# Banded attention as one pipeline over 16 blocks, with pairs of heads on the two halves of the TensorE array

## The reference

```python
def _windowed_gqa(h, pos, w_qkv, sink, w_o):
    qkv = h @ w_qkv
    q, k, v = jnp.split(qkv, [1024, 1280], axis=-1)      # 16 q heads, 4 k heads, 4 v heads, 64 wide
    # per query block of 128 tokens: keys of the block before, its own, the block after
    scores = jnp.einsum('bnqkgd,bnskd->bnkgqs', q * 64 ** -0.5, kb)
    scores = scores - slopes * dist                      # ALiBi by distance of positions
    scores = jnp.where(mask, scores, NEG)                # |t - s| <= 128
    p = jax.nn.softmax(jnp.concatenate([scores, sink_col], axis=-1), axis=-1)[..., :-1]
    return jnp.einsum('bnkgqs,bnskd->bnqkgd', p, vb).reshape(B, S, 1024) @ w_o
```

## Time and profile before

| | |
|---|---|
| Median of 3 runs | 1250.61 us (1248.01 to 1251.63) |
| The profiled execution's own time | 1250.18 us |
| Span of its profile | 1248.4 us, so 1.8 us lie around it |
| TensorE busy | 1191.3 us, 95% |
| VectorE, ScalarE, GpSimd busy | 630.4, 354.0, 399.0 us |
| Mean granted TensorE clock | 0.990 |
| TensorE share of the chain that ended last | 80%, DVE 9% |

### The profile page before, as it was taken

How to read it: one execution, slowest core, us unless ns; L and a number is a source line. 1 busy time by engine, 2 the same in 40 slices (tenths; PEclk the granted TensorE clock), 3 DMA queues, 4 the chain that set the end, 5 groups by cost and what they waited for, 6 DMA issues and landing times.

```text
span 1248.4 us, 18246 instructions
## 1 busy us (share of the span) xinstructions
PE 1191.3 (95%) x5796; PEld 992.8 (80%) x5796; DVE 630.4 (50%) x1067; ACT 354.0 (28%) x689; POOL 399.0 (32%) x415
## 2 busy tenths in 40 slices
PE   6899999999999999999889999899999999999996
PEld 5788878788888888888867777678788888888885
DVE  6777764433333433454576776744443333343432
ACT  4266652222200111111365665632222200111101
POOL 3343335333311333343241412325233311323342
PEclk8999999999999999999989999999999999999998
DMA  6211113232433233333200101013333332333421
GB/s 161 68 34 35 35 34 101 85 99 86 119 93 89 87 101 101 109 93 91 70 20 18 36 0 34 18 39 114 97 89 101 103 115 68 101 96 89 120 81 67
DMA packets 176475, 96.67 MB, mean 77 GB/s; under 512 B 8752, under 2 KB 173104, under 8 KB 176432
## 3 DMA queue, kind: packets, MB, share of 16 engines
q1 hardware_dynamic: 176432, 96.12, 26.5%
HBM read 94.01 MB, written 2.10 MB: 77 GB/s over the span
## 4 chain that ended last, share of the span: by engine, by line
PE 80%; DVE 9%; issue 4%; ACT 3%; POOL 2%; DMA 1%; ACTq 0%; DVEq 0%; POOLq 0%; SPq 0%
PE bank L949 26%; PE bank L951 25%; PE bank L950 25%; PE bank L1391 2%; DVE w_lo L1473 1%; POOL w_hi L442 1%; DVE stat L2004 1%; DVE apt_lo L1666 1%; PE bank L1088 1%; DVE s_a L1658 1%; DVE bpt_lo L2009 1%; DMA x_n<-in_x 1%; ACT s_b L880 1%; ACT bpt_hi L886 0%; DVE w_lo L1490 0%
## 5 line engine op out<-in xcount | busy, mean ns | idle before, releaser
L1473 DVE TENSOR_TENSOR w_lo<-w_raw,w_hi 128x1024 fp32r<-128x1024 f32 (+2 forms) x151 | 203.2, 1346 | 297.8 <-POOL w_hi L442 297.7
L442 POOL TENSOR_SCALAR w_hi<-w_raw 128x1024 fp32r<-128x1024 f32 (+3 forms) x159 | 183.3, 1153 | 421.4 <-PE bank L951 410.0
L949 PE MATMUL bank<-x_hi,w_lo 128*128 128x512 f32 x784 | 308.3, 393 | 9.9 <-DVE w_lo L1473 7.7
L951 PE MATMUL bank<-x_hi,w_hi 128*128 128x512 f32 x784 | 306.3, 391 | 0.0
L950 PE MATMUL bank<-x_lo,w_hi 128*128 128x512 f32 x784 | 306.3, 391 | 0.0
L949 PEld LDWEIGHTS bank<-x_hi,w_lo 128*128 128x128 f32 x784 | 147.8, 189 | 42.1 <-DVE w_lo L1473 5.5
L951 PEld LDWEIGHTS bank<-x_hi,w_hi 128*128 128x128 f32 x784 | 147.7, 188 | 30.9
L950 PEld LDWEIGHTS bank<-x_lo,w_hi 128*128 128x128 f32 x784 | 148.0, 189 | 29.7
L949 PE MATMUL bank<-f_hi,w_lo 128*128 128x512 f32 x352 | 137.8, 391 | 1.0 <-DVE f_lo L1776 1.0
L951 PE MATMUL bank<-f_hi,w_hi 128*128 128x512 f32 x352 | 137.1, 389 | 0.0
L950 PE MATMUL bank<-f_lo,w_hi 128*128 128x512 f32 x352 | 137.0, 389 | 0.0
(11 more groups left out here) (219 smaller groups left out, 1863.6 us busy)
## 6 DMA issues: line engine op xcount, KB each, us to landing
w_raw<-in_ffn_w_gu SPq DMA_DIRECT2D x88, 512.0 KB, 3.8
w_raw<-in_ffn_w_down SPq DMA_DIRECT2D x32, 704.0 KB, 4.4
w_raw<-in_a_w_qkv SPq DMA_DIRECT2D x12, 512.0 KB, 3.8
w_raw<-in_a_w_o SPq DMA_DIRECT2D x8, 512.0 KB, 3.6
w_raw<-in_b_w_o SPq DMA_DIRECT2D x8, 512.0 KB, 3.8
w_raw<-in_b_w_in SPq DMA_DIRECT2D x4, 672.0 KB, 4.0
w_raw<-in_b_w_uq SPq DMA_DIRECT2D x4, 576.0 KB, 4.0
x_n<-in_x SPq DMA_DIRECT2D x4, 512.0 KB, 5.3
```

The costliest lines, as they stand in the source:

```text
L442: pool.tensor_scalar(split_part(w_hi, s, cols, kv), raw_part(s, cols, kv), 1.0, 1.0, ALU.mult, ALU.mult) \
L949: pe.matmul(o, ll, rh, start=start, stop=False)
L951: return pe.matmul(o, lh, rh, start=False, stop=stop)
L1473: dve.tensor_tensor(split_part(w_lo, s, cols, kv), raw_part(s, cols, kv), f(split_part(w_hi, s, cols, kv)), ALU.subtract) \
```

## The change

What it does:

- The two loops over groups and query blocks become one list of 16 blocks, b = 4 x group + n. TensorE issues the scores of block b, then the transposes of block b-1, then a few projection steps (`a_filler`), then the values of block b-1 piece by piece, with further steps between. Where n = 0, the second pair of heads is scored behind the transposes. Scores use four banks (0, 1, 2, 7).
- The key tiles are stored without zeros: `ks` holds key heads as the projection left them (even head on partitions 0 to 63, odd on 64 to 127), `kx` the same with the halves exchanged, filled by four DMAs from SBUF to SBUF. A score matmul reads 64 partitions only; the even head's and the odd head's matmuls alternate, so they stand on different halves of the array.
- The query projections 0 and 1 get buffers of their own, loaded right behind the key weights, and run before the value projection. All query tiles are double-buffered (`aq_hi[:, g % 2]`).
- V is projected token block by token block, with all key blocks of the contraction together, into banks 6 and 5, and is written directly to `av_hi` and `av_lo` for all groups at once. The scores of block 0 stand behind its first quarter.
- The low parts of queries 2 to 7 and of three query and output weights move from DVE to POOL. Reciprocals are taken for two heads at once. An early exponential loads ACT's table. The masks `near` are made before the keys are evicted, and lie in unused ends of the weight slots.

```diff
-            def a_group(g, last):
-                def scores(u):
...
-                    q = (slice(None), hd // 2, slice(n * P, (n + 1) * P))
-                    k = (slice(None), hd % 2, slice(k0 * P, (k0 + nk) * P))
-                    product(banks[u % 3][:, 0:nk * P], aq_hi[q], aq_lo[q], kp_hi[k], kp_lo[k], True, True) \
-                        .then_inc(s_done, 1)
...
+            def a_scores(b, i):
...
+                for k_low, q_low in ((False, True), (True, False), (False, False)):
+                    for odd in range(2):
+                        rows = slice(odd * HD, (odd + 1) * HD)
+                        q = (aq_lo if q_low else aq_hi)[rows, g % 2, i, n * P:(n + 1) * P]
+                        here = odd == g % 2
+                        kt = (ks_lo if here else kx_lo) if k_low else (ks_hi if here else kx_hi)
+                        ins = pe.matmul(banks[A_SCORE_BANKS[2 * i + odd]][:, 0:nk * P], q,
+                                        kt[rows, g // 2, k0 * P:(k0 + nk) * P],
+                                        start=q_low, stop=not (k_low or q_low))
+                        if not (k_low or q_low):
+                            ins.then_inc(s_done, 1)
...
+            for b in range(1, A_BLOCKS + 1):
+                n = b % NT
+                nk = a_keys(b - 1)[1]
+                steps = a_filler(b)
...
+                if b < A_BLOCKS:
+                    a_scores(b, 0)
+                    if n:
+                        a_scores(b, 1)
+                if b == A_BLOCKS:
+                    fill(3)
+                elif n == 3:
+                    fill(KD)
+                a_turn(b - 1, 0)
+                a_turn(b - 1, 1)
+                if n == 0 and b < A_BLOCKS:
+                    a_scores(b, 1)
+                fill(2 if b < A_BLOCKS else 1)
+                a_values(b - 1, 0)
+                if nk > 2:
+                    a_turn(b - 1, 2)
+                fill(1)
+                a_values(b - 1, 1)
+                fill(KD)
+                if nk > 2:
+                    a_values(b - 1, 2)
...
+            sp.wait_ge(ks_ready, 2)
+            for src, dst in ((ks_hi, kx_hi), (ks_lo, kx_lo)):
+                for half in range(2):
+                    there, here = slice((1 - half) * HD, (2 - half) * HD), slice(half * HD, (half + 1) * HD)
+                    sp.dma_start(f(dst[there, :, :]), f(src[here, :, :])).then_inc(kx_in, 16)
...
+                if g < GROUPS - 1:
+                    c = C_Q + 2 * g
+                    if n == 3 if g == 0 else n == 2:
+                        a_q_lo(2 * g + 2)
+                        w_split_hi(c // 2 + 1, 0, W_COLS)
+                    if n == 3:
+                        a_q_lo(2 * g + 3)
+                        a_w_lo(c + 2)
+                if g and n == 0:
+                    w_split_hi(C_Q // 2 + g, 1, W_COLS)
```

More of the change, by code:

```diff
@@ new lines, in a_turn @@
+            def a_turn(b, i):
+                unit = a_unit(b, i)
+                if b == 0 and i < 2:
+                    pe.wait_ge(q_tmp_ready, i + 1)
+                else:
+                    pe.wait_ge(pt_free, unit - 1)
+                for j, hd in enumerate((0, 2, 1, 3)):
+                    if i == 0 and j != 2:
+                        pe.wait_ge(p_ready, 4 * b + hd + 1)
+                    last = pe.transpose(banks[3 + unit % 2][:, j * P:(j + 1) * P],
+                                        s_a[:, b % 2, hd, 1 + i * P:1 + (i + 1) * P], ident[:])
+                last.then_inc(pt_done, 1)
@@ new lines, in a_values @@
+            def a_values(b, i):
+                k0, nk = a_keys(b)
+                pe.wait_ge(pt_free, a_unit(b, i) + 1)
+                if i == 0:
+                    pe.wait_ge(o_free, O_A + b)
+                    if b == 0:
+                        pe.wait_ge(av_zero, 2)
+                        pe.wait_ge(v_ready, NT)
+                for odd in range(2):
+                    at = (2 * (b // NT) + 1 - odd) * HD
+                    v = (slice(None), k0 + i, slice(at, at + P))
+                    p = (slice(None), b % 2, i, slice(2 * P * odd, 2 * P * (odd + 1)))
+                    last = product(banks[5][:, 0:2 * P], av_hi[v], av_lo[v], apt_hi[p], apt_lo[p],
+                                   i == 0 and odd == 0, i == nk - 1 and odd == 1)
+                if i == nk - 1:
+                    last.then_inc(o_done, 1)
@@ L1730, in _ @@
-            for g in range(GROUPS - 1):
-                a_group(g, False)
-            a_group(GROUPS - 1, True)
             def add_to_h(c, bank_s, m, used, dst=None):
```

719 lines of the change are left out of this document (352 added, 367 removed).

## The result

The change takes 1261.26 us (median of 6 runs, 1259.48 to 1265.82) beside 1251.12 for the kernel before on the same chip: ratio 1.0086, 95% interval 1.0068 to 1.0103. It is **10 us slower**, where 1246.2 was forecast, and outside the range of 1239 to 1254.

What follows compares the result with a forecast made beforehand. TensorE, busy 95% of the span, was taken as the bound. First stretch 3.5 us less, two middle groups 1.0 less, last group 0.1 more: 1250.18 - 4.4 = 1245.8, median 0.4 higher, so 1246.2; range 1239 to 1254.

Steps and rivals of the forecast that it cites:

- the term for the waits of the new order: Block-by-block walk through the engines' queues in the changed stage: 20.6 us of TensorE waits, each handover counted in full.
- Last group: Blocks 12 to 15: own work 25.6, waits 6.7, output split 0.3, together 32.6 us, 0.1 more than before.
- Blocks with n = 3: Fourth query block of a group: own work 6.9 us, wait of 1.3 for the third transposes' copies before the last values.
- the two weight splits: Block 1: splits on POOL and DVE hold up the maxima and first probabilities, a wait of 3.6 us.
- n = 0: First query block of a group: own work 6.1 us, wait of 0.8 for a weight split moved to POOL.
- n = 1 and 2: Second and third query blocks: own work 6.2 and 7.2 us, wait of 0.9 in each before the values.
- the pairs: Score matmuls of even and odd heads: one spacing a pair, 0.173 or 0.118 us, 13.9 us less.
- the visits: Entering and leaving the half-height mode for scores: 19 times at 0.25 us, 4.8 us in all.
- the copies from SBUF to SBUF: Four new 256 KB key copies before block 0's scores: cost nothing, or 5 us if as slow as loads.
- pairs one after the other: Rival: paired score matmuls do not overlap, scores cost 13.9 us more, total 1255.9, slower; chance 0.12.
- drains: Rival: each entry and exit of half-height mode costs 0.70 us together, +6.8, total 1253.0, no measurable change; chance 0.14.
- The marks named: Signs to check: paired starts, 0.9 us apt_lo waits, block 1 near 53 us, twelfth output product near 175; wrong if groups exceed 31.

Runs made afterwards that it cites:

- the run with the steps around them: The change with half of the projection steps of n = 3 blocks moved from ahead of the transposes to later places: 1257.7 us, ratio 1.0050.
- the run with the heads in turn: The change with each pair's score products issued as three of one head, then three of the other, instead of alternating: 1262.0 us, ratio 1.0089.
- The late split: The change with half the n = 3 projection steps behind the transposes and the second query-weight slot's split behind block 1's maxima: 1255.1 us, ratio 1.0035.
- scores_twice: The change with every pair's three score products computed twice, 14 us more of TensorE's time: 1268.5 us, ratio 1.0138.
- the runs with both pairs ahead: The change with block b+1's scores ahead of block b-1's last values, half the n = 3 steps behind transposes: 1253.6 us; later runs keep both edits.
- the pairs' run in the old order: The kernel before, own order of work kept, only the score products issued in pairs on the two halves of the rows: 1251.9 us, ratio 1.0003.
- the reordered kernel: The change with scores issued earlier and projection steps, weight splits, query readout and output steps moved: 1247.5 us, ratio 0.9969.

## Why the prediction was wrong

- **The step that failed** is the term for the waits of the new order. "My walk has 20.6 us of waits" was too small by some 13 us, of which the clock is about 2. The forecast was 3.9 us a middle group over own work of 26.4; the groups took 34.2 and 32.5, so 7.8 and 6.1. From block 1 to block 4: 33.0 us in place of 28.9. Last group 35.6 in place of 32.6. With 0.4 up to block 1, these make, to rounding, the 13.4 us between the forecast stage (145.7) and the measured one. By place:
  - Blocks with n = 3: the walk waited only for the third copy. All projection steps stand ahead of the transposes, so the first two copies are bare as well; 1.2 to 1.3 us a block over the forecast (blocks 3, 7, 11). Shown by the run with the steps around them for blocks 7 and 11, which got 1.2 shorter; block 3 got 0.4 shorter and block 4 1.4. (The walk's own terms, 0.28 + 0.59 + 0.75 + 0.69 less 0.7, also make 1.6 and not the 1.3 written.)
  - Block 1 took 12.2, not 9.8, of which 1.5 is the clock; without its fall (the run with the heads in turn) it took 10.7, so the two weight splits cost 4.5 in place of 3.6. The late split shows that they are what block 1 waits for.
  - n = 0: block 4 took 8.7, not 6.9, with waits of 1.6 for w_lo and 0.4 for aq_lo; blocks 8 (7.0) and 12 had 0.4 for w_lo. The walk had one subtraction and the split ahead of the scaling of block 4; at the end of group 0 four stand there, two aq_lo, w_hi and w_lo, from 84.73 to 90.59:

```profile
84.73 1.28 POOL L549 TENSOR_TENSOR aq_lo<-q_tmp,aq_hi 128x512 fp32r<-128x512 f32 x1
85.97 1.05 POOL L479 TENSOR_SCALAR w_hi<-w_raw 128x1024 fp32r<-128x1024 f32 x1
86.98 1.29 POOL L549 TENSOR_TENSOR aq_lo<-q_tmp,aq_hi 128x512 fp32r<-128x512 f32 x1
88.21 2.38 POOL L543 TENSOR_TENSOR w_lo<-w_raw,w_hi 128x1024 fp32r<-128x1024 f32 x1
```

  So POOL was late by its queue and not by its speed: its subtractions took the 1.29 and 2 x 1.29 forecast, or less. (The 1.29 and 1.87 of the earlier trace rows are a multiplication and an addition, not subtractions.) Moving w_hi and w_lo ahead cut block 4 by 1.5.
  - n = 1 and 2: right to 0.5 us (7.4 in blocks 5 and 9, 8.6 and 8.5 in 6 and 10, beside 7.1 and 8.1). The 0.66 ahead of block 8's values stands for the 0.9 forecast.
  - The last group's 3.0 us is not broken down. Block 15's fall of the clock is in it: from its scores to the end of the stretch the change takes 15.5 us at a clock of 0.89, scores_twice, with 0.7 us more work there, 15.1 at 1.00.
- **The clock** was in no term. In the run with the heads in turn the same block 1 kept a clock of 1.00 and took 10.7 us, so the fall costs 1.5 there; block 15's costs 0.4 to 1.1 by the comparison above, together 1.9 to 2.6 us, an estimate. In the runs with both pairs ahead block 15's does not occur.
- **What the pairs' run in the old order adds.** It is no proof against the sum, which was for the new order; but it shows where such a saving goes: half into entering and leaving, the rest into waits, here for banks.
- **Right:** the pairs (one spacing, so 13.9 us less), the visits nearly (0.29 beside 0.25, 0.8 us more over 19), block 1 at 53.35 (forecast 53.4), the copies from SBUF to SBUF unseen, V's evictions hidden, the rest of the kernel unchanged within 0.7. The rule of the Trainium skill (TensorEngine Tiling (Array Packing), Key Properties) that a change of mode drains TensorE agrees with the late starts, 0.20 us on entering and 0.09 on leaving. The rivals "pairs one after the other" and "drains" (0.70 a visit) fall. The first had the right sign and, with 1255.9, half of the loss, by a mechanism that isn't there.
- The marks named were met in part: twelfth product at 188.6, not 175; groups over 31 us, which was said to make the forecast wrong.

**Settled:** the loss is order, not work. Moving instructions alone took 14.3 us from the change by the medians and 16.2 from the stretch, at the same count of TensorE's matmuls. **Open:** what the pairs are worth in the reordered kernel. An added 14 us of scores cost 11.8 there, but full-height scores would also save the 19 visits (5.5 us), so some 6 us is an estimate; the reordered kernel with full-height scores was not run. Which chain holds the old order at 30.8 us, with banks enough for the pairs, was not tried either.

## What to carry to other kernels

Before counting an engine's saved time, ask what would hold the order if that engine were faster: the cheap test is to save the time in the old order first, and to look whether the edit that saves it brings waits of its own, as the pairs did here with the banks. In a software pipeline, follow one block around through every in-order queue and ask what the *first* instruction of the next block stands behind: here scores behind the last values, then q_tmp ahead of the maxima, then a weight split ahead of the normalisations. Walk every instruction of each queue: the walk here left two of POOL's out. Whatever waits for another engine belongs behind what is ready, and filler belongs where the waits are, not where the program text has a gap.

## What was not expected of the hardware

Matmuls on different halves of the rows need not be neighbours in the program: three of one head ran beside the three of the next, starts 0.01 us apart, in the same time as when they alternated (0.17 a pair at 384 columns). So did their weight loads: the fourth matmul's began at 55.42, the second's at 55.52. The Trainium skill (PSUM — Partial Sum Buffer, Engine vs sequencer instructions) says that matmuls start and complete in program order; for two sets of rows this trace differs. And the clock's fall after a stall was not the same each time. In the run with the heads in turn block 1 begins 2.06 us later in the profile. In the same 4 us of the block TensorE was busy for the same 1.39 us, but the clock stayed at 1.00 there and in the 4 us behind, where in the change it fell to 0.50:

```profile
60.06:64.06 4.00, 1.39 (x9) 0.95 (x9) 3.38 (x11) 3.46 (x10) 1.16 (x2) 1.00 0.91 251
```

What decides between the two, no run here shows.
